# Stick-breaking heads: the suffix products in two one-pass parts

## Chip, cores, metric

The kernel runs on one core of one Trainium2 chip. The metric is the device time of one execution in microseconds (us), the median of several runs. The engines are TensorE (PE: matmuls), VectorE (DVE), ScalarE (ACT), GpSimd (POOL) and SyncE (SP: it issues the loads).

## The reference, cut to what matters

The program is a transformer: a first block, then a second block of two layers, all in float32. The change lies in the first layer of the second block, in the eight heads of the stick-breaking attention:

```python
z = jnp.einsum('bqhd,bshd->bhqs', qb, k, preferred_element_type=F32) * scale
past = key_pos[None, :] < qpos[:, None]
log_keep = jnp.where(past, jax.nn.log_sigmoid(-z), 0.0)
suffix = lax.cumsum(log_keep, axis=3, reverse=True) - log_keep
w = jnp.where(past, jnp.exp(jax.nn.log_sigmoid(z) + suffix), 0.0)
return jnp.einsum('bhqs,bshd->bqhd', w.astype(v.dtype), v)
```

There are 512 positions and 64 channels in a head. The exponent of a weight is z less the sum of softplus(z) over the key itself and all later keys. The same layer also has eight heads of a sparse attention (DSA), which see only the 128 highest-scored keys of each query; choosing them (the top-k) is independent of the stick-breaking heads.

## The kernel before, in words

**Order of work.** Every engine has its own instruction list, written out by hand in one long function, and engines wait for each other on semaphores alone. Nothing is reordered when it runs: an instruction that waits holds up all that stands behind it on its engine.

**The layout of a head.** The scores of a head are held transposed (keys on the 128 partitions, queries along the free axis), in four key tiles. Only queries from the key tile on matter, so they are 512, 384, 256 and 128 columns wide, 1280 in all. They live in PSUM in one of two regions of three banks (`region(h)`, by h % 2). In SBUF, `zw` and `spt` each have two buffers of 128x1280, again by h % 2.

**One head, step by step.**
- `sb_scores(h)` (TensorE, L1106 to L1121): three products of split operands and one mask product for each key tile. It waits until the Exp of head h-2 has read the region, and raises `z_rd`.
- `sb_softplus(h)` (ScalarE, L1757 to L1766): Abs, Exp and Ln, 128x1280 each, into `zw`.
- `sb_max(h)` (VectorE, L2569 to L2573): max(z, 0) + `zw`, which is softplus(z), into `spt`. It waits for the Ln, and for the value products of head h-2 (`sv_rd`), since these read the same buffer of `spt`. It raises `sp_rd`.
- `sb_suffix(h)` (TensorE, L1123 to L1132): ten float32 matmuls with `negtri` (a triangle of -1) or `negone` (all -1) as one operand and `spt` as the other, 2560 columns in all, added onto the scores in PSUM. They wait for `sp_rd` and raise `arg_rd`. The trace shows two matmul records for each.
- The Exp (ScalarE, L1779) reads the region and writes the weights over `spt`; it raises `wgt_rd`.
- `sb_values(h)` (TensorE, L1134 to L1142): twenty products of 64 columns; raises `sv_rd`. `sb_out(h)` (VectorE, L2575 to L2578) copies the result out.

**The lists of the stage.** On TensorE the loop over heads (L1171 to L1187) runs suffix(h), values(h-1), scores(h+2); with h = 1 and 3 transposes of the next pair's queries and keys stand in between (`sb_job`), with h = 5 those of the DSA (`dsa_job`). On ScalarE (L1778 to L1790) it runs Exp(h), then for h = 1, 3, 5 copies that round the transposed queries and keys to the 32-bit matmul format `fp32r` (`sb_high`, `job_high`), then softplus(h+2). On VectorE (L2589 to L2612) it runs max(h+1), the low parts of the queries and keys (`sb_low`), out(h-1), and then up to four rounds of the top-k (`topk`), for h < 4 mixed with `sum_step(13, ...)`, a step of the modulation vectors. The 25 top-k rounds of this loop end in `select`, which writes the last masks `Mk` (L2413) and raises `msk_rd`. Here the loop body of h is called cycle h; on VectorE it begins at max(h+1).

**Ahead of the loop**, ScalarE runs softplus(0), softplus(1), `sb_high(3)` and `split_high(NC1 + 11)` (L1532, the rounded part of a weight chunk that is used after the attention), and VectorE runs max(0), `sb_low(2)`, `sb_low(3)` (L2556, L2557) and `split_low(NC1 + 11)` (L2043).

**Behind the loop** stands the DSA. TensorE runs its first scores, waits for three masks (`msk_rd`, L1227), runs its second scores and then values(7); VectorE follows with the maxima and the copies. The kernel goes on from there with the output projection and the feed-forward layers.

Other products of this kernel already use split operands: ScalarE's Copy into an `fp32r` tile gives the rounded part, and VectorE subtracts that from the full value to give the rest, in `fp32r` too:

```python
A(uH[:, k], X[:, k % 3, :], ACT.Copy)
V.tensor_tensor(uL[:, k], X[:, k % 3, :], uH[:, k].bitcast(F32), ALU.subtract)
```

`overlay` gives out SBUF addresses from the current position and takes none up, so a tile named in it lies on top of what is allocated next.

Of the kernel before, what the change touches and what calls it, by code (L numbers as in the profile page):

```python
# [6 lines left out]
ALU = mybir.AluOpType  # L7
# [141 lines left out]
def program(nc, t, out):  # L149
    ctx = ExitStack()  # L150
    with ctx:
# [8 lines left out]
        with ExitStack() as o:  # L160
# [70 lines left out]
        rp_rd, odd_rp, zero_rd, ixT, ix_hi, ix_lo, ixs_rd, ixr_rd, ix_acc, msk_rd = [sem(n) for n in (  # L231
            "rp_rd", "odd_rp", "zero_rd", "ixT", "ix_hi", "ix_lo", "ixs_rd", "ixr_rd", "ix_acc", "msk_rd")]
        jobT, job_hi, job_lo = sem("jobT"), sem("job_hi"), sem("job_lo")
        z_rd, zmin_rd, zexp_rd, zln_rd, sp_rd, arg_rd, wgt_rd, sv_rd, so_rd = [sem(n) for n in (
            "z_rd", "zmin_rd", "zexp_rd", "zln_rd", "sp_rd", "arg_rd", "wgt_rd", "sv_rd", "so_rd")]
        ds_rd, dmx_rd, dp_rd, dt_rd, dpv_rd, do_rd = [sem(n) for n in ("ds_rd", "dmx_rd", "dp_rd", "dt_rd", "dpv_rd", "do_rd")]
        dpt_rd = [sem("dpt_rd0"), sem("dpt_rd1")]
        aoT, ao_hi, ao_lo = sem("aoT"), sem("ao_hi"), sem("ao_lo")
# [56 lines left out]
        def s2(name, shape, dt=F32):  # L295
# [18 lines left out]
        ixr, = overlay([("ixr", [P, 2, SEQ], F32)])  # L314
        ixH, ixL, izH, izL = overlay([("pad_iz", [P, 1024], F32)] + [(n, [P, 2, SEQ], F32R) for n in
                                                                     ("ixH", "ixL", "izH", "izL")])[1:]
        zw = s2("zw", [P, 2, 1280])
        spt = s2("spt", [P, 2, 1280])
        e2.close()


# [395 lines left out]
        def _(pe):  # L717
# [403 lines left out]
                last.then_inc(z_rd, 1)  # L1121

            def sb_suffix(h):  # L1123
                z, s_ = region(h), spt[:, h % 2]
                pe.wait_ge(sp_rd, h + 1)
                for kt in range(4):
                    for k2 in range(kt, 4):
                        w = SEQ - k2 * P
                        o0 = ZOFF[kt] + (k2 - kt) * P
                        last = mm(z[:, o0:o0 + w], negtri[:] if k2 == kt else negone[:], s_[:, ZOFF[k2]:ZOFF[k2] + w],  # L1130
                                  start=False, stop=True, skip_group_check=True)
                last.then_inc(arg_rd, 1)  # L1132

            def sb_values(h):  # L1134
# [376 lines left out]
        def _(act):  # L1511
# [255 lines left out]

            sb_high(0)
            sb_high(1)
            even_tile_out(4, 0)  # L1770
            sb_softplus(0)
            even_tile_out(4, 2)
# [1 line left out]
            sb_softplus(1)  # L1774
            sb_high(3)
            split_high(NC1 + 11)
            for h in range(NH):
                act.wait_ge(arg_rd, h + 1)  # L1778
                A(spt[:, h % 2], region(h), ACT.Exp).then_inc(wgt_rd, 1)  # L1779
                if h in (1, 3):  # L1780
                    sb_high(h + 3)
                if h == 5:
                    act.wait_ge(z_rd, h + 1)
                    job_high(8, 0, 7, True)
                if h + 2 < NH:
                    sb_softplus(h + 2)
                if h in (1, 3):
                    sb_high(h + 4)
                if h == 5:
                    job_high(9, 0, 7, False)  # L1790
# [241 lines left out]
        def _(dve):  # L2032
# [536 lines left out]
            def sb_max(h):  # L2569
# [2 lines left out]
                    dve.wait_ge(sv_rd, h - 1)  # L2572
                V.scalar_tensor_tensor(spt[:, h % 2], region(h), 0.0, zw[:, h % 2], ALU.max, ALU.add).then_inc(sp_rd, 1)  # L2573

            def sb_out(h):  # L2575
                dve.wait_ge(sv_rd, h + 1)
                V.tensor_copy(T0[:, :, h * HD:h * HD + HD], ps[:, 3, 0:256].rearrange("p (t d) -> p t d", t=4))\
                    .then_inc(so_rd, 1)  # L2578
# [6 lines left out]
            even_tile_out(4, 3)  # L2585
            sb_low(2)
            sb_low(3)
            split_low(NC1 + 11)
            for h in range(NH):  # L2589
                steps = range(TOPK_SB[h], TOPK_SB[h + 1])  # L2590
# [8 lines left out]
                for kt in range(4):  # L2599
                    if h < 4 and kt % 2 == 0:  # L2600
                        sum_step(13, 2 * h + kt // 2)
                    if kt == 1 and h in SB_TURN:
                        group_columns(SB_TURN[h])
                    if kt < len(steps) - 1:
                        topk(steps[kt])
                if h in (1, 3):
                    sb_low(h + 4)
                if h == 5:
# [421 lines left out]
```

## Time and profile before

| | us |
|---|---|
| median of 3 runs | 1778.62 |
| lowest, highest | 1777.19, 1778.79 |
| the profiled execution | 1773.95 |
| its span in the trace | 1772.2 |
| the stage, from the first suffix product to the last mask | 487.7 to 568.0 |

All times below are microseconds from the start of the span of the profiled execution. A view by stretch gives for each engine its busy time and the number of its instructions, then the clock that was granted to TensorE and the DMA load. A timeline row gives start, duration, engine, line, operation, output and inputs with shapes, and in brackets how long the engine had been idle and what released it. The durations of neighbouring VectorE instructions overlap a little, so what an instruction takes from its engine is the distance to the next start where nothing waits.

### The profile page before, as it was taken

Reading aid. Unit: us, or ns where it says so; the run is one execution under the profiler, and the core shown is the slowest. Engines: PE = TensorE matmul, PEld = TensorE weight load, DVE = VectorE, ACT = ScalarE, POOL = GpSimd, SP = SyncE. Lnnn points to the kernel's source line nnn. Section 1 sums busy time; section 2 is a strip of 40 time slices with the busy share of each in tenths; the row PEclk is TensorE's granted clock in tenths of the full one; section 3 lists DMA queues with packets and bytes.
Section 4 is the critical chain, followed back from the end, with each engine's and each line's share of the span. In section 5 each row is a group of like instructions: output and inputs, shape, how many; then the busy total and the mean of one; then the engine's idle time right before and its main releaser. Section 6 shows DMA issues by size and latency. Waiting matters only on the chain.

```text
span 1772.2 us, 22785 instructions
## 1 busy us (share of the span) xinstructions
PE 1666.1 (94%) x8951; PEld 1367.0 (77%) x8957; DVE 1012.6 (57%) x1433; ACT 656.8 (37%) x887; POOL 335.5 (19%) x260
## 2 busy tenths in 40 slices
PE   4999999999988998999999999899879899999999
PEld 3898787888777876888887887677657688888877
DVE  3578798877877758433333447656666733333243
ACT  4422566433363523433332224334453533333121
POOL 0000000000000004788884011224411000000011
PEclk9999999999998998999999999999989999999999
DMA  8645200442210333465554322212002232332321
GB/s 283 202 146 188 95 1 1 135 169 84 83 60 13 96 119 107 147 196 182 185 189 137 118 89 76 96 48 72 24 25 75 64 98 95 97 99 98 118 84 48
DMA packets 145605, 188.00 MB, mean 106 GB/s; under 512 B 6925, under 2 KB 104565, under 8 KB 145524
## 3 DMA queue, kind: packets, MB, share of 16 engines
q1 hardware_dynamic: 145524, 186.88, 32.8%
q8 instruction: 55, 0.90, 0.2%
q14 instruction: 26, 0.21, 0.0%
HBM read 184.77 MB, written 2.10 MB: 105 GB/s over the span
## 4 chain that ended last, share of the span: by engine, by line
PE 59%; DVE 14%; POOL 9%; issue 6%; DMA 5%; ACT 4%; SPq 1%; another core or an unknown queue 0%; POOLq 0%; DVEq 0%; ACTq 0%
PE ps L836 7%; PE ps L837 7%; PE ps L838 7%; POOL mraw L619 4%; POOL msum L626 4%; DMA mraw<-in_w_mod_dram 3%; PE ps L1339 2%; PE ps L1346 2%; PE ps L1340 2%; PE ps L1347 2%; PE ps L1343 2%; PE ps L1348 2%; PE ps L1402 2%; PE ps L1404 2%; PE ps L1403 2%
## 5 line engine op out<-in xcount | busy, mean ns | idle before, releaser
L1532 ACT ACTIVATE whi<-wraw 128x2048 fp32r<-128x2048 f32 x71 | 135.8, 1913 | 312.0 <-PE ps L838 215.4
L2043 DVE TENSOR_TENSOR wlo<-wraw,whi 128x2048 fp32r<-128x2048 f32 x64 | 148.2, 2315 | 154.7 <-ACT whi L1532 154.6
L2794 DVE TENSOR_TENSOR wlo<-wraw,whi 128x2048 fp32r<-128x2048 f32 x22 | 51.7, 2350 | 203.2 <-ACT whi L1892 203.2
L1339 PE MATMUL ps<-uH,whi 128*128 128x512 f32 x352 | 141.4, 402 | 9.8 <-ACT uH L1860 8.3
L836 PE MATMUL ps<-hH,whi 128*128 128x512 f32 x352 | 140.7, 400 | 0.0
L1340 PE MATMUL ps<-uH,wlo 128*128 128x512 f32 x352 | 139.9, 397 | 0.0
L837 PE MATMUL ps<-hL,whi 128*128 128x512 f32 x352 | 139.8, 397 | 0.0
L838 PE MATMUL ps<-hH,wlo 128*128 128x512 f32 x352 | 139.6, 397 | 0.0
L1346 PE MATMUL ps<-uH,whi 128*128 128x512 f32 x352 | 136.9, 389 | 0.0
L1347 PE MATMUL ps<-uL,whi 128*128 128x512 f32 x352 | 136.9, 389 | 0.0
L1348 PE MATMUL ps<-uH,wlo 128*128 128x512 f32 x352 | 136.9, 389 | 0.0
L1343 PE MATMUL ps<-uL,whi 128*128 128x512 f32 x352 | 111.4, 398 | 3.9 <-DVE uL L2733 3.9
L626 POOL TENSOR_TENSOR msum<-msum,mraw 128x512 f32<-128x512 f32 x66 | 107.5, 1628 | 5.2
L836 PE MATMUL ps<-uH,whi 128*128 128x512 f32 x256 | 103.0, 402 | 0.0
L837 PE MATMUL ps<-uL,whi 128*128 128x512 f32 x256 | 100.2, 392 | 0.0
L838 PE MATMUL ps<-uH,wlo 128*128 128x512 f32 x256 | 100.2, 392 | 0.0
L619 POOL TENSOR_TENSOR mraw<-mraw,cpad 128x1024 f32<-128x1024 f32 x44 | 84.9, 1930 | 55.4 <-PE ps L751 42.5
L1896 ACT ACTIVATE whi<-wraw 128x2048 fp32r<-128x2048 f32 x22 | 42.2, 1919 | 138.3 <-PE ps L1348 138.3
L1889 ACT ACT_TABLE_LOAD x22 | 28.2, 1283 | 173.0 <-PE ps L1343 172.9
L2110 DVE SCALAR_TENSOR_TENSOR cy<-utp,cols,cy 128x512 f32<-128x512 f32 x116 | 87.1, 751 | 3.4
L1339 PEld LDWEIGHTS ps<-uH,whi 128*128 128x128 f32 x352 | 67.9, 193 | 26.2 <-issue 12.1
L653 POOL TENSOR_TENSOR sqd<-sqd 128x512 f32<-128x512 f32 x2 | 2.8, 1384 | 434.5 <-ACT sqd L1833 434.5
(500 smaller groups left out, 3910.5 us busy)
## 6 DMA issues: line engine op xcount, KB each, us to landing
mraw<-in_w_mod_dram SPq DMA_DIRECT2D x104, 512.0 KB, 3.8
wraw<-in_w_gate_dram SPq DMA_DIRECT2D x22, 1024.0 KB, 5.3
wraw<-in_w_up_dram SPq DMA_DIRECT2D x22, 1024.0 KB, 5.4
wraw<-in_w_down_dram SPq DMA_DIRECT2D x16, 1024.0 KB, 5.2
wraw<-in_w_in_dram SPq DMA_DIRECT2D x11, 1024.0 KB, 5.4
mfirst<-in_w_mod_dram SPq DMA_DIRECT2D x16, 512.0 KB, 7.5
wraw<-in_w_in_even_dram SPq DMA_DIRECT2D x8, 1024.0 KB, 5.8
wraw<-in_w_in_odd_dram SPq DMA_DIRECT2D x16, 512.0 KB, 4.5
```

The costliest lines, as they stand in the source:

```text
L619: g.tensor_tensor(w, w, cpad[:, 2 * kp:2 * kp + 2, 2:3].to_broadcast([P, 2, GW]), ALU.mult).then_inc(msum_rd, 1)
L626: g.tensor_tensor(msum[:], msum[:], w[:, kk], ALU.add).then_inc(msum_rd, 1)
L836: mm(o, h, xh[:, k0 + k], start=(first and k == 0), stop=False)
L837: mm(o, h, xl[:, k0 + k], start=False, stop=False)
L838: last = mm(o, l, xh[:, k0 + k], start=False, stop=(done and k == nk - 1))
L1339: mm(o[m], w_[0][m][:, k], uH[:, k], start=(k == 0), stop=False)
L1340: mm(o[m], w_[1][m][:, k], uH[:, k], start=False, stop=False)
L1343: last = mm(o[m], w_[0][m][:, k], uL[:, k], start=False, stop=(k == KT - 1))
L1346: mm(o[m], w_[0][m][:, k], uH[:, k], start=(k == 0), stop=False)
L1347: mm(o[m], w_[0][m][:, k], uL[:, k], start=False, stop=False)
L1348: last = mm(o[m], w_[1][m][:, k], uH[:, k], start=False, stop=(k == KT - 1))
L2043: V.tensor_tensor(wlo[:, n % 2, :], wraw[:, n % 2, :], whi[:, n % 2, :].bitcast(F32), ALU.subtract).then_inc(lo_done, 1)
```

## The change

The softplus values `spt` are split before the suffix products. ScalarE copies them to `spH` (type `fp32r`), VectorE subtracts `spH` from `spt` and writes `spL` (also `fp32r`), and TensorE runs the ten suffix matmuls twice, first on `spH`, then on `spL`, with `fp32r` copies of the triangle and of the ones (`rtri`, `rone`). `spH` lies on the addresses of `zw`, `spL` on those of `spt`. The matmuls on `spH` wait for the copy, those on `spL` for the subtraction.

The copy of head h+1 stands on ScalarE behind Exp(h) and the copies that follow it, and ahead of softplus(h+2); that of head 0 stands behind `split_high(NC1 + 11)`. The subtraction of head h+1 stands on VectorE behind the first top-k round of cycle h; that of head 0 stands between `sb_low(3)` and `split_low(NC1 + 11)`. The two small copies `rtri` and `rone` stand on ScalarE behind `sb_high(1)`.

```diff
+        spH, spL = overlay([("spH", [P, 2, 1280], F32R), ("spL", [P, 2, 1280], F32R)])
         zw = s2("zw", [P, 2, 1280])
         spt = s2("spt", [P, 2, 1280])
+        rtri = s2("rtri", [P, P], F32R)
+        rone = s2("rone", [P, P], F32R)
...
             def sb_suffix(h):
-                z, s_ = region(h), spt[:, h % 2]
-                pe.wait_ge(sp_rd, h + 1)
-                for kt in range(4):
-                    for k2 in range(kt, 4):
-                        w = SEQ - k2 * P
-                        o0 = ZOFF[kt] + (k2 - kt) * P
-                        last = mm(z[:, o0:o0 + w], negtri[:] if k2 == kt else negone[:], s_[:, ZOFF[k2]:ZOFF[k2] + w],
-                                  start=False, stop=True, skip_group_check=True)
+                z = region(h)
+                if h == 0:
+                    pe.wait_ge(tri_rd, 1)
+                for part in range(2):
+                    s_ = (spH, spL)[part][:, h % 2]
+                    pe.wait_ge((sph_rd, spl_rd)[part], h + 1)
+                    for kt in range(4):
+                        for k2 in range(kt, 4):
+                            w = SEQ - k2 * P
+                            o0 = ZOFF[kt] + (k2 - kt) * P
+                            last = mm(z[:, o0:o0 + w], rtri[:] if k2 == kt else rone[:], s_[:, ZOFF[k2]:ZOFF[k2] + w],
+                                      start=False, stop=(part == 1), skip_group_check=True)
                 last.then_inc(arg_rd, 1)
...
             sb_high(0)
             sb_high(1)
+            act.wait_ge(rp_rd, 1)
+            A(rtri[:], negtri[:], ACT.Copy)
+            A(rone[:], negone[:], ACT.Copy).then_inc(tri_rd, 1)
             even_tile_out(4, 0)
...
             split_high(NC1 + 11)
+            def sb_part(h):
+                act.wait_ge(sp_rd, h + 1)
+                A(spH[:, h % 2], spt[:, h % 2], ACT.Copy).then_inc(sph_rd, 1)
+
+            sb_part(0)
             for h in range(NH):
                 act.wait_ge(arg_rd, h + 1)
                 A(spt[:, h % 2], region(h), ACT.Exp).then_inc(wgt_rd, 1)
...
+                if h + 1 < NH:
+                    sb_part(h + 1)
                 if h + 2 < NH:
                     sb_softplus(h + 2)
...
+            def sb_rest(h):
+                dve.wait_ge(sph_rd, h + 1)
+                V.tensor_tensor(spL[:, h % 2], spt[:, h % 2], spH[:, h % 2].bitcast(F32), ALU.subtract).then_inc(spl_rd, 1)
...
             sb_low(3)
+            sb_rest(0)
             split_low(NC1 + 11)
             for h in range(NH):
...
                     if kt < len(steps) - 1:
                         topk(steps[kt])
+                    if kt == 0 and h + 1 < NH:
+                        sb_rest(h + 1)
```

## Rows read from the trace of the kernel before

**Rows 1.** Page, section 1: busy time of each engine over the span.

```profile
PE 1666.1 (94%) x8951; PEld 1367.0 (77%) x8957; DVE 1012.6 (57%) x1433; ACT 656.8 (37%) x887; POOL 335.5 (19%) x260
```

**Rows 2.** Busy time by stretch: cycles 1 to 4, cycles 5 and 6.

```profile
505.50:543.30 37.80, 36.23 (x225) 29.10 (x224) 36.56 (x69) 21.46 (x20) 0.00 (x0) 1.00 0.23 70
543.30:568.00 24.70, 21.10 (x129) 17.17 (x127) 20.88 (x39) 9.04 (x9) 0.00 (x0) 0.93 0.00 1
```

**Rows 3.** Waits between 470 and 590 us: who waited for whom; us, times, longest.

```profile
DVE spt L2573 <- PE ps L1141: 5.8, 3, 2.8
...
PE ps L1117 <- DVE uL L2557: 4.6, 2, 4.2
```

**Rows 4.** Timeline of VectorE: start us, duration us, engine, line, operation.

```profile
493.08 0.69 DVE L2557 TENSOR_TENSOR uL<-ps,uH 64x512 fp32r<-64x512 f32 x1
494.32 2.29 DVE L2043 TENSOR_TENSOR wlo<-wraw,whi 128x2048 fp32r<-128x2048 f32 x1 [0.54 <-ACT whi L1532]
496.64 1.49 DVE L2573 SCALAR_TENSOR_TENSOR spt<-ps,zw 128x1280 f32<-128x1280 f32 x1
...
505.54 1.49 DVE L2573 SCALAR_TENSOR_TENSOR spt<-ps,zw 128x1280 f32<-128x1280 f32 x1 [2.73 <-PE ps L1141]
...
525.85 1.49 DVE L2573 SCALAR_TENSOR_TENSOR spt<-ps,zw 128x1280 f32<-128x1280 f32 x1
...
536.99 1.49 DVE L2573 SCALAR_TENSOR_TENSOR spt<-ps,zw 128x1280 f32<-128x1280 f32 x1
...
538.73 0.69 DVE L2398 MAX8 m<-work 128x8 f32<-128x512 f32 x1
...
542.63 0.68 DVE L2400 MATCH_REPLACE8 work<-m,work 128x512 f32<-128x512 f32 x1
546.12 1.49 DVE L2573 SCALAR_TENSOR_TENSOR spt<-ps,zw 128x1280 f32<-128x1280 f32 x1 [2.82 <-PE ps L1141]
...
556.28 1.49 DVE L2573 SCALAR_TENSOR_TENSOR spt<-ps,zw 128x1280 f32<-128x1280 f32 x1 [0.24 <-PE ps L1141]
...
567.56 0.43 DVE L2413 TENSOR_SCALAR Mk<-work 128x512 bf16<-128x512 f32 x1
```

**Rows 5.** Timeline of TensorE, from the score products to the first value products.

```profile
485.16 0.39 PE L1118 MATMUL ps<-uL,uH 128*128 128x512 f32 x1
485.38 0.40 PE L1119 MATMUL ps<-uH,uL 128*128 128x512 f32 x1
...
486.93 0.27 PE L1118 MATMUL ps<-uL,uH 128*128 128x128 f32 x1
487.04 0.28 PE L1119 MATMUL ps<-uH,uL 128*128 128x128 f32 x1
...
487.67 1.02 PE L1130 MATMUL ps<-spt,negtri 128*128 128x512 f32 x2
...
495.69 0.47 PE L1117 MATMUL ps<-uH 128*128 128x512 f32 x1 [3.52 <-ACT spt L1779]
...
498.19 1.12 PE L1130 MATMUL ps<-spt,negtri 128*128 128x512 f32 x2
...
503.06 2.34 PE L1141 MATMUL ps<-T,spt 128*128 128x64 f32 x20
```

**Rows 6.** Timeline of ScalarE around the first head.

```profile
488.70 1.27 ACT L1764 ACTIVATE zw<-zw 128x1280 f32<-128x1280 f32 x1
...
492.38 1.91 ACT L1532 ACTIVATE whi<-wraw 128x2048 fp32r<-128x2048 f32 x1
```

**Rows 7.** TensorE by stretch: length, busy us, granted clock (1.00 is 2.4 GHz, 0.50 is 1.2).

```profile
472.00:476.00 4.00, 1.32 (x3) 0.69 0.00 0
476.00:480.00 4.00, 4.00 (x16) 0.50 0.00 0
492.00:496.00 4.00, 0.48 (x3) 1.00 0.01 2
556.00:560.00 4.00, 2.32 (x6) 0.85 0.01 2
```

More of the change, by code:

```diff
@@ L233, in program @@
         jobT, job_hi, job_lo = sem("jobT"), sem("job_hi"), sem("job_lo")
-        z_rd, zmin_rd, zexp_rd, zln_rd, sp_rd, arg_rd, wgt_rd, sv_rd, so_rd = [sem(n) for n in (
-            "z_rd", "zmin_rd", "zexp_rd", "zln_rd", "sp_rd", "arg_rd", "wgt_rd", "sv_rd", "so_rd")]
+        z_rd, zmin_rd, zexp_rd, zln_rd, sp_rd, arg_rd, wgt_rd, sv_rd, so_rd, sph_rd, spl_rd, tri_rd = [sem(n) for n in (
+            "z_rd", "zmin_rd", "zexp_rd", "zln_rd", "sp_rd", "arg_rd", "wgt_rd", "sv_rd", "so_rd", "sph_rd", "spl_rd", "tri_rd")]
         ds_rd, dmx_rd, dp_rd, dt_rd, dpv_rd, do_rd = [sem(n) for n in ("ds_rd", "dmx_rd", "dp_rd", "dt_rd", "dpv_rd", "do_rd")]
```

## Prediction

> **What bounds the kernel now.** I read four views in this order. The page says that TensorE is busy for 94% of the span [rows 1], which invites the thought that any TensorE time saved is time saved. So the busy time by stretch comes next. The stage with the suffix products runs from 487.67 [rows 5] to the last mask, which ends at 567.99 (567.56 + 0.43) [rows 4]. In its middle, 505.5 to 543.3, VectorE is busy 36.56 us of 37.8 and TensorE 36.23: two engines are full at once. Behind it, to 568.0, VectorE has 20.88 of 24.7 [rows 2]. The waits tell which is the limit where. VectorE waited for value products three times in the stage, 5.8 us together [rows 3], and the timeline puts these waits at the starts of cycles 1, 5 and 6 (2.73, 2.82 and 0.24 us ahead of max). Between 505.54 and 543.31 (542.63 + 0.68) it had none [rows 4]. So cycles 1 to 4 are VectorE's. The stage itself ends when VectorE has finished its top-k: the DSA's second scores wait for the last mask, and values(7), and all later work, stand behind them on TensorE. Whatever VectorE does more in a full cycle shifts that mask.
>
> TensorE spends on one suffix stream, with four transposes behind it, 4.87 us (498.19 to 503.06) [rows 5], about 4.4 without them. That is what the change shortens.
>
> **The change part by part.**
>
> *The suffix streams.* With `fp32r` operands, score matmuls start 0.22 us apart at 512 columns and 0.11 apart at 128 [rows 5]. For 384 and 256 I take 0.17 and 0.14, a little under and about on the straight line. One stream has 1, 2, 3 and 4 matmuls of 512, 384, 256 and 128 columns: 0.22 + 0.34 + 0.42 + 0.44 = 1.4 us. Two streams take 2.8 in place of 4.4, so TensorE saves 1.6 us a head, 13 in all. In the cycles that VectorE fills this is worth nothing.
>
> *The copy on ScalarE.* SBUF to SBUF, 1280 columns, costs 1.27 us as Exp [rows 6]. The PSUM variants are no dearer, so both ends lie at about 1.25 and I take 1.27. In a cycle it lies beside TensorE's score products. These take 2.5 us (495.69 to 498.19) [rows 5] and begin no later than max does, so the high stream starts some 3.0 us after max starts (1.49 + 0.1 + 1.27 + 0.1; 0.1 is my estimate of a hand-over, of which the trace shows 0.03 from 494.29 on ScalarE [rows 6] to 494.32 on VectorE [rows 4]). Behind the copy only softplus(h+2) is queued. It ends at about 6.8, which is long ahead of the next max. The two small copies ahead of the loop fall where ScalarE has time, and I cost them at nothing. Without that cover they would cost two instructions well under 1.27.
>
> *The subtraction on VectorE.* It has not run at this size. The nearest row above is max itself: two inputs, 1280 columns, 1.49 us. The subtraction of 2048 columns takes 2.29 and one of 512 takes 0.69 [rows 4], and the line between these gives 1.49 again. Starts follow some 0.07 sooner than ends, so I take 1.42 a piece. As a lower bound I use 0.8, should 1280 columns run at about half that price. The upper bound is 1.5.
>
> *The head of the stage.* Before, suffix(0) could start at 487.67, as soon as softplus was there. Now the copy of head 0 stands on ScalarE behind `split_high`, which ends at 494.29 [rows 6]. The copy ends at 495.6. TensorE has nothing to do for 8 us, from about 487.6 to 495.7. The longest wait for L2557, 4.2 us [rows 3], ends in the stretch from 472 to 476, where the granted clock was 0.69; over the next 4 us it was 0.50, the 1.2 GHz level. The wait of 3.52 us ahead of 495.69 [rows 5] left it at 1.00 [rows 7]. An idle time of 8 is beyond both, so I take suffix(0) at the low clock: 2 x 2.8, end at 501.3. Then Exp(0) to 502.65 and score products to 505.25. Suffix(1) takes 2.8 to 508.05, the transposes 0.45, the value products 2.34 [rows 5], and max(2) starts at 510.95 where it started at 505.54 [rows 4]: **+5.4**. At full clock suffix(0) ends at 498.5 and all this comes 2.7 sooner. VectorE doesn't set it: the subtraction of head 0 ends at 497.1, `split_low` 2.3 later, max(1) at 500.85, and what is left of cycle 0 is done by 508.5.
>
> *Cycles 1 to 3* took 31.45 us (505.54 to 536.99) [rows 4] without idle time and get one subtraction each: **+4.3**.
>
> *Cycle 4.* VectorE reached 543.31 and waited until 546.12. Now the chain runs: max and the copy out 1.74, one top-k round 1.52 (a third of the 4.58 from 538.73 to 543.31) [rows 4], subtraction 1.49, hand-over 0.1, low stream 1.4, transposes 0.45, value products 2.34. The sum is 9.05, against 9.13 before: **-0.1**. Here the shorter streams pay for the subtraction and the wait for it.
>
> *Cycles 5 and 6* are full once the 0.24 us wait is gone: 2 x 1.42 - 0.24 = **+2.6**. In each full cycle the low stream waits for the subtraction, about 5 us after max starts, but TensorE then has 2 to 3 us in hand before the next max needs its buffer.
>
> *Behind the stage* nothing changes, and nothing there has the time to absorb a late mask, so the shift stays. No transfer is added or moved, and SP's and POOL's lists are unchanged.
>
> **The sum:** 5.4 + 4.3 - 0.1 + 2.6 = +12.2 us. The profiled execution took 1773.95, so its like would take 1786.1. That execution lies 4.7 under the median of 1778.62. Against the median the sum gives 1790.8, and that is my number.
>
> **A rule on the clock.** The Trainium skill, page "TensorE: Matmul & The Clock Gate", section "HAM oscillation — how this bites in real kernels", says that a loop with an idle wait in each round can find its matmuls slowed in each round. By it the sum would be that of the second rival below. The trace agrees in part: the idle time of 3.52 us left the clock alone, the 4.2 did not.
>
> **The rivals.**
>
> *No fall at the head.* Suffix(0) runs at full clock. For it speaks the wait of 3.52 us that left 1.00 [rows 7]; against it, that the new one is over twice as long. 12.2 - 2.7 = +9.5: 1788.1.
>
> *A fall in every cycle.* In each cycle TensorE would be idle for 2 to 4 us in several pieces. Over 556 to 560, with 2.32 us busy of 4, the clock went down to 0.85 [rows 7], so short pieces can do it. A fall as at 472 to 480 lasts (0.31 + 0.50) x 4 / 0.5 = 6.5 us and costs TensorE half of that, 3.2. In cycles 1 to 3 and 5 some 2.5 of it are covered, which leaves 0.6 each. In cycle 4 nothing is covered. That adds 4 x 0.6 + 3.2 = 5.6, for +17.8: 1796.4. Against it speaks that over all of cycles 1 to 4 the clock stood at 1.00 [rows 2], though with fuller work.
>
> *TensorE is the limit, and the kernel gets faster.* The place is the start of a cycle, max(h+1) behind the value products. If the shorter streams took away the three waits of 5.8 us [rows 3], and the subtractions and the head fell into time that VectorE has over, the mask would come 5.8 us sooner: 1772.8. It decides where VectorE is idle for more than 1.42 us in a cycle. It was so in cycles 0 and 4 alone, and the head delay takes the first.
>
> *The shift is taken up later.* Some wait behind the mask, on a transfer or on ScalarE, would have to be as long as 12 us. It would give 1778 to 1781. None of the views read shows one.
>
> *The streams are not one-pass.* If a matmul with `fp32r` copies took as long as one with float32, both streams would cost 4.4. The chain of a cycle would then be 12 us or more, the head over 6 more, about +23 in all: 1802. The score matmuls' 0.22 us speaks against it.
>
> **How the numbers follow.** Forecast 0.43, no fall 0.22, a fall in every cycle 0.19, faster 0.05, taken up later 0.07, not one-pass 0.04. The range begins at the case without a fall with cheaper subtractions (9.5 less 5 x 0.6 = 6.5, so 1785) less 1 for the scatter of the runs (1777.19 to 1778.79): 1784. It ends at the fall in every cycle with the same scatter: 1798. A measurement can tell about 0.2%, 3.6 us, from no change. With 0.01 moved to each of the first two from the slower cases, which hold 0.88, faster by more has 0.06, within has 0.08, slower has 0.86.
>
> **What would show it.** Right: the two suffix streams of a head at 1.4 us each at full clock. Subtractions of 1.49 us, eight of them. The first suffix matmul at 495.7 with a granted clock near 0.5. Cycle 1 beginning at about 511, cycles 1 to 3 of 11.5 to 12.6 us with no idle time on VectorE, and the last mask at about 580. The head step is wrong if the clock over 496 to 501 is 1.00 (mask at about 577.5). The step on the full cycles is wrong if max waits for value products again in cycles 2, 3 or 4: then the chain over ScalarE and TensorE is longer than I have it. The whole is wrong if the mask is late and the end is not.

## Result and profile after

The changed kernel takes 1791.23 us in the median of 4 runs (1788.30 to 1792.39); the kernel before, timed beside it, 1777.90 (1775.05 to 1778.79). The ratio is 1.0076, with a 95% interval from 1.0059 to 1.0092: 13 us slower. The profiled execution took 1792.3 us, its span 1790.5.

The page of the changed kernel, section 1, answers to [rows 1]:

```profile
PE 1670.1 (93%) x8957; PEld 1374.6 (77%) x8957; DVE 1023.9 (57%) x1441; ACT 667.1 (37%) x897; POOL 333.1 (19%) x260
```

TensorE is busy for 4 us more (1666.1 before), though its streams are cheaper; a busy time counts matmuls at the low clock at their full length. VectorE has 11.3 us more (1012.6 before) and ScalarE 10.3 (656.8). These are the eight subtractions, which take 1.41 us each from VectorE's time (8 x 1.41 = 11.3), and the ten copies, whose durations add up to 10.8 us and overlap their neighbours a little.

VectorE's timeline of the changed kernel answers to [rows 4]; L2591 is max, L2595 the subtraction, L2431 the mask:

```profile
487.82 1.49 DVE L2591 SCALAR_TENSOR_TENSOR spt<-ps,zw 128x1280 f32<-128x1280 f32 x1 [5.53 <-ACT zw L1773]
...
500.22 1.49 DVE L2595 TENSOR_TENSOR spL<-spt,spH 128x1280 fp32r<-128x1280 f32 x1 [1.70 <-ACT spH L1790]
...
503.95 1.49 DVE L2591 SCALAR_TENSOR_TENSOR spt<-ps,zw 128x1280 f32<-128x1280 f32 x1
...
508.22 1.49 DVE L2595 TENSOR_TENSOR spL<-spt,spH 128x1280 fp32r<-128x1280 f32 x1 [1.26 <-ACT spH L1790]
...
515.19 1.49 DVE L2591 SCALAR_TENSOR_TENSOR spt<-ps,zw 128x1280 f32<-128x1280 f32 x1 [2.44 <-PE ps L1148]
```

```profile
550.84 1.49 DVE L2591 SCALAR_TENSOR_TENSOR spt<-ps,zw 128x1280 f32<-128x1280 f32 x1
...
554.09 1.49 DVE L2595 TENSOR_TENSOR spL<-spt,spH 128x1280 fp32r<-128x1280 f32 x1
...
560.01 1.49 DVE L2591 SCALAR_TENSOR_TENSOR spt<-ps,zw 128x1280 f32<-128x1280 f32 x1 [1.46 <-PE ps L1148]
...
571.36 1.49 DVE L2591 SCALAR_TENSOR_TENSOR spt<-ps,zw 128x1280 f32<-128x1280 f32 x1
...
584.05 0.43 DVE L2431 TENSOR_SCALAR Mk<-work 128x512 bf16<-128x512 f32 x1
```

The subtraction takes 1.49 us, and the next instruction starts 1.41 later (501.63, 509.63 in the same view). The subtractions of heads 0 and 1 wait for their copies (1.70 and 1.26 us); no later one does. Read the starts of max as the beats of the stage. The third of them is the start of cycle 1, the sixth (550.84) that of cycle 4. Max never waits between 515.19 and 550.84; it waits for value products (L1148) at cycles 1 and 5, and no longer at cycle 6. The parts of the stage, from the start of max(0) to the end of the last mask:

| part of the stage (us) | before | predicted change | changed | measured change | second trace of the changed kernel |
|---|---|---|---|---|---|
| head, max(0) to max(2) | 22.25 | +5.4 | 27.37 | +5.12 | 27.02 |
| cycles 1 to 3 | 31.45 | +4.3 | 35.65 | +4.20 | 35.64 |
| cycle 4 | 9.13 | -0.1 | 9.17 | +0.04 | 9.19 |
| cycles 5 and 6, to the mask | 21.87 | +2.6 | 24.47 | +2.60 | 24.46 |
| stage | 84.70 | +12.2 | 96.66 | +11.96 | 96.31 |

TensorE's timeline shows the two streams, first of head 0, then of head 1, then of head 2; it answers to [rows 5]:

```profile
500.34 0.76 PE L1137 MATMUL ps<-spH,rtri 128*128 128x512 f32 x1 [7.76 <-ACT spH L1790]
...
502.92 0.73 PE L1137 MATMUL ps<-spL,rtri 128*128 128x512 f32 x1
...
509.47 0.47 PE L1137 MATMUL ps<-spH,rtri 128*128 128x512 f32 x1
...
510.88 0.44 PE L1137 MATMUL ps<-spL,rtri 128*128 128x512 f32 x1
...
518.04 0.50 PE L1137 MATMUL ps<-spH,rtri 128*128 128x512 f32 x1
...
520.98 0.50 PE L1137 MATMUL ps<-spL,rtri 128*128 128x512 f32 x1 [1.34 <-DVE spL L2595]
```

In head 1 the streams start 1.41 us apart, the predicted 1.4. In head 0 they start 2.58 apart, after 7.76 us of idle time. In head 2 the second one waits 1.34 us for VectorE, as predicted for the full cycles. The clock over the head, in pieces of 4 us (length, busy, granted clock), answers to [rows 7]:

```profile
492.00:496.00 4.00, 0.58 (x6) 0.93 0.00 0
496.00:500.00 4.00, 0.00 (x0) 0.50 0.00 0
500.00:504.00 4.00, 3.66 (x14) 0.50 0.02 4
504.00:508.00 4.00, 2.58 (x13) 0.79 0.00 0
```

It is at 0.50, the level of 1.2 GHz, from before 496 until after 504, where the kernel before had 1.00.

**Where the rest of the 18 us between the two profiled executions is.** The difference of their spans is 18.3 us. max(0) starts at 487.82 and not at 483.29: 4.5 us, all of it ahead of the stage, where only the two small copies (0.6 us) are new. In the second trace of the changed kernel it starts at 483.12, so this is scatter between executions. The stage gives 11.96. From the mask to the last output copy of the DSA it is 61.27 against 60.03: 1.2, which goes with the clock, as the traces below show. The rest, 0.6, lies behind. The medians, 13.3 apart, agree with stage and tail together.

### The profile page after: what moved, and what is told of

It is laid out like the page before. It is cut to its first block, busy times and chain, and to the rows that moved or that the text cites. A ratio compares the mean times of both kernels' runs of the same rounds, so it can differ in the third digit from the quotient of the medians.

```text
span 1790.5 us, 22816 instructions
## 1 busy us (share of the span) xinstructions
PE 1670.1 (93%) x8957; PEld 1374.6 (77%) x8957; DVE 1023.9 (57%) x1441; ACT 667.1 (37%) x897; POOL 333.1 (19%) x260
## 4 chain that ended last, share of the span: by engine, by line
PE 60%; DVE 14%; POOL 9%; issue 7%; DMA 4%; ACT 4%; SPq 1%; POOLq 0%; DVEq 0%; ACTq 0%
PE ps L839 7%; PE ps L841 7%; PE ps L840 7%; POOL mraw L622 4%; POOL msum L629 4%; DMA mraw<-in_w_mod_dram 3%; PE ps L1346 2%; PE ps L1353 2%; PE ps L1355 2%; PE ps L1347 2%; PE ps L1350 2%; PE ps L1354 2%; PE ps L1409 2%; PE ps L1411 2%; PE ps L1410 2%
## 5 line engine op out<-in xcount | busy, mean ns | idle before, releaser
L1346 PE MATMUL ps<-uH,whi 128*128 128x512 f32 x352 | 140.9, 400 | 10.6 <-ACT uH L1878 8.3
```

The costliest lines, as they stand in the source:

```text
L1346: mm(o[m], w_[0][m][:, k], uH[:, k], start=(k == 0), stop=False)
```

## Experiments

All times of parts are read from VectorE's timeline as in the table above. "Stage" is from the start of max(0) to the end of the last mask, "tail" from there to the last output copy of the DSA.

| kernel | head | cycles 1-3 | cycle 4 | cycles 5, 6 | stage | tail | median of runs |
|---|---|---|---|---|---|---|---|
| before | 22.25 | 31.45 | 9.13 | 21.87 | 84.70 | 60.03 | 1777.9 to 1779.5 |
| changed | 27.37 | 35.65 | 9.17 | 24.47 | 96.66 | 61.27 | 1791.2 |
| changed, second trace | 27.02 | 35.64 | 9.19 | 24.46 | 96.31 | 61.17 | 1790.1 (one run) |
| split of head 0 forward | 22.26 | 35.66 | 10.17 | 24.46 | 92.55 | 61.07 | 1787.5 |
| no subtractions | 26.41 | 31.76 | 9.09 | 21.65 | 88.91 | 57.06 | 1781.3 |
| second stream unread | 27.44 | 35.64 | 12.26 | 24.46 | 99.80 | 62.16 | 1794.7 |
| second stream cut | 25.72 | 35.64 | 12.80 | 24.45 | 98.61 | 61.32 | 1792.1 |
| second stream cut, again | 25.98 | 35.65 | 7.91 | 24.45 | 93.99 | 60.94 | 1786.1 (one run) |
| TensorE kept busy in the head | 26.00 | 35.66 | 12.25 | 24.46 | 98.37 | 62.06 | 1789.1 |
| subtractions on GpSimd | 23.28 | 34.17 | 10.37 | 21.65 | 89.47 | 62.69 | 1786.2 |
| float32, rounds moved | 23.47 | 29.26 | 9.78 | 18.83 | 81.34 | 58.64 | 1771.0 |
| float32, rounds moved, Exp first | 20.55 | 29.27 | 9.78 | 18.83 | 78.43 | 56.86 | 1768.0 |
| split, rounds moved | 23.52 | 32.97 | 10.02 | 20.38 | 86.89 | 56.90 | 1779.4 |
| split, rounds moved, Exp first | 21.53 | 36.22 | 10.18 | 20.40 | 88.33 | 57.50 | 1775.6 |

**The head: the place of the first copy.**

```diff
             sb_high(2)
+            sb_part(0)
             sb_softplus(1)
             sb_high(3)
             split_high(NC1 + 11)
-            sb_part(0)
...
             sb_low(2)
+            sb_rest(0)
             sb_low(3)
-            sb_rest(0)
             split_low(NC1 + 11)
```

> The changed kernel with the split of head 0 moved forward: its copy stands on ScalarE ahead of softplus(1), its subtraction on VectorE ahead of the low parts of the keys. I measure the stage from the start of max(0) to the end of the last mask: 84.70 us in the kernel before, 96.66 in the changed one. My theory (VectorE's list is the limit in the full cycles, and the head is late because the copy stands behind the weight split): suffix(0) ends before Exp(0) can run anyway, so the head costs nothing, max(2) comes 22.3 us after max(0) (27.4 in the changed kernel, 22.3 before), the clock stays at full speed over the head, and the stage takes 91.6. Whole time some 5 us under the changed kernel, 8 over the one before. Rival (the place of the copy does not matter, TensorE and ScalarE wait for each other in every cycle alike): stage within 1 us of 96.7.

The head fell to 22.26 us, that of the kernel before to 0.01. The ratio to the kernel before is 1.0036 (1.0025 to 1.0048), against 1.0076. So the +5.1 goes away with the place of the first split (its copy and its subtraction). The stage came out at 92.55 and not 91.6, since cycle 4 took 1.0 us more; in this trace TensorE's clock was 0.50 from 545 to 548, in the midst of it. The clock over the head stayed at full speed only until 492, and that part of the expectation was wrong:

```profile
487.00:492.00 5.00, 3.57 (x29) 1.00 0.02 3
492.00:497.00 5.00, 1.27 (x3) 0.65 0.00 0
...
545.00:548.00 3.00, 3.00 (x14) 0.50 0.00 0
```

The agreement to 0.01 us is a balance of two differences, and luck. After a wait of 5.16 us for Exp(0) the score products ran at the low clock: 4.37 us (495.73 to 500.10), against 2.50 in [rows 5].

```profile
495.70:500.30 4.60, 4.57 (x17) 0.50 0.00 0
```

```profile
495.73 0.77 PE L1120 MATMUL ps<-uH 128*128 128x512 f32 x1 [5.16 <-ACT spt L1795]
...
500.10 0.60 PE L1137 MATMUL ps<-spH,rtri 128*128 128x512 f32 x1
```

```profile
498.21 1.27 ACT L1787 ACTIVATE spH<-spt 128x1280 fp32r<-128x1280 f32 x1 [2.62 <-DVE spt L2591]
```

So suffix(1) started 16.39 us after max(0), and 14.90 after it in the kernel before: 1.49 later. Its two streams took 2.93 us (to 503.03) where the float32 stream took 4.44 (498.19 to 502.63): 1.51 shorter. Up to 0.6 of the 1.49 is the clock. The other 0.9 is the copy of head 1, which ended at 499.48 (498.21 + 1.27), so no score product could have brought suffix(1) ahead of that. Here the shorter streams pay for the new copy on the path, and for the low clock.

**VectorE's time: with and without subtractions.**

```diff
-                    s_ = (spH, spL)[part][:, h % 2]
-                    pe.wait_ge((sph_rd, spl_rd)[part], h + 1)
+                    s_ = spH[:, h % 2]
+                    pe.wait_ge(sph_rd, h + 1)
...
-            sb_rest(0)
...
-                    if kt == 0 and h + 1 < NH:
-                        sb_rest(h + 1)
```

> The changed kernel without the eight subtractions: the second stream reads the rounded part again, so the remainder is left out and the rounded part counts twice. All copies and all matmuls stay. My theory: cycles 1 to 3 go back to 31.5 us together (35.65 in the changed kernel), cycle 4 takes 8.7 (9.17), cycles 5 and 6 take 21.6 (24.47), the head stays late, so the stage takes 89.1, 7.5 less than the changed kernel. Rival (the loss is in TensorE's idle waits for the copies and in its clock, not in VectorE's time): the cycles stay at over 11 us each and the stage at 94 or more.

Stage 88.91 against 89.1 expected; the parts missed by more than the sum, the head by -0.9 us, cycles 1 to 3 by +0.3 and cycle 4 by +0.4. TensorE and ScalarE had the work of the changed kernel, copies and both streams, and still cycles 1 to 3 went back to 31.8 us. The ratio to the kernel before is 1.0011 (0.9994 to 1.0028). Its counterpart keeps the subtractions too, and only lets the second stream read the rounded part:

```diff
-                    s_ = (spH, spL)[part][:, h % 2]
-                    pe.wait_ge((sph_rd, spl_rd)[part], h + 1)
+                    s_ = spH[:, h % 2]
+                    if part == 0:
+                        pe.wait_ge(sph_rd, h + 1)
                     for kt in range(4):
+                        if part and kt == 3:
+                            pe.wait_ge(spl_rd, h + 1)
```

> The changed kernel with all copies, subtractions and both full streams, but the second stream reads the rounded part again, and only its last matmul waits for the subtraction; the remainder is left out and the rounded part counts twice. Against the run without subtractions it differs by VectorE's work alone. My theory: cycles 1 to 3 take 35.65 us and cycles 5 and 6 take 24.46, as in the changed kernel (31.76 and 21.65 without subtractions). Cycle 4 tells about the miss with the cut second stream (12.80 us where 7.9 was expected): there the clock stood at 0.50, and here TensorE has 1.3 us more work in each head with the same waits. If the clock was the cause, cycle 4 takes 7.9 to 9.2. Rival (a wait that I don't see): 12.8 again.

Cycles 1 to 3 took 35.64 us and cycles 5 and 6 took 24.46, the changed kernel's numbers. Between these two runs lie 3.9 us over three cycles and 2.8 over two, that is 1.3 to 1.4 for each subtraction, and 1.41 is what one takes from VectorE's time. This is the clearest pair of the study: same matmuls, same copies, and the subtractions on VectorE make the difference. (The last matmul of a head waits for its subtraction here, but max never waited for value products in cycles 1 to 3, so that wait was not on the path.) Cycle 4, however, took 12.26 us and not 7.9 to 9.2, with TensorE busy throughout at a clock of 0.61.

**TensorE's time: a shorter second stream.**

```diff
                         for k2 in range(kt, 4):
+                            if part and kt < 3:
+                                continue
```

> The changed kernel with the second stream cut to its last matmul, of 128 columns: the remainder of three key tiles of four is left out. Copies and subtractions stay. This takes about 1.3 us of TensorE from each head (2.4 from head 0, at the low clock). My theory: nothing changes in cycles 1, 2, 3, 5 and 6; the head gets 3.7 to 3.9 shorter and cycle 4 gets 1.3 shorter, so the stage takes 91.5. Rival (TensorE's streams are on the path in every cycle): each head gives 1.3 and more, 10 to 11 in all, and the stage takes 86.

Cycles 1, 2, 3, 5 and 6 didn't move by more than 0.02 us, though TensorE had 1.3 us less work in each. Its time didn't fall with the work: over cycles 1 to 3 it was busy for 28.31 us at a clock of 0.77, against 26.61 at 0.99 in the changed kernel. That the beat held even so shows that TensorE's time doesn't set it, and the rival of a gain in every head falls. But two parts missed. The head gave 1.65 us, not 3.7: the score products started 2.4 us sooner and suffix(1) took 1.3 less, but the score products ran at the low clock and took 4.34 us (502.45 to 506.79) instead of 2.36 (507.11 to 509.47 in the changed kernel). Cycle 4 got 3.6 us longer where it should have got 1.3 shorter. VectorE's row says for whom it waited, and the windows say why that was late:

```profile
559.70 1.49 DVE L2593 SCALAR_TENSOR_TENSOR spt<-ps,zw 128x1280 f32<-128x1280 f32 x1 [4.95 <-PE ps L1150]
```

```profile
546.90:550.00 3.10, 3.10 (x15) 0.50 0.00 0
550.00:553.00 3.00, 3.00 (x14) 0.50 0.00 0
553.00:556.00 3.00, 3.00 (x16) 0.50 0.03 5
556.00:559.70 3.70, 3.70 (x18) 0.50 0.00 0
```

TensorE was busy all the time in cycle 4, at half clock from end to end. The same kernel once more, to see whether that belongs to it:

> The kernel with the cut second stream once more, unchanged: does the long cycle 4 come again? The remainder of three key tiles of four is left out. If the clock falls wherever TensorE has too little to do in the full cycles: cycle 4 above 11 us again and the granted clock near 0.5 in it. If it was chance in one execution: 7.9 to 9.2.

```profile
544.75:552.66 7.91, 7.88 (x58) 0.88 0.00 0
```

```profile
544.75 1.49 DVE L2593 SCALAR_TENSOR_TENSOR spt<-ps,zw 128x1280 f32<-128x1280 f32 x1
...
552.66 1.49 DVE L2593 SCALAR_TENSOR_TENSOR spt<-ps,zw 128x1280 f32<-128x1280 f32 x1 [0.20 <-PE ps L1150]
```

Cycle 4 took 7.91 us, the 7.9 worked out from rows, at a mean clock of 0.88. The very same instructions had taken 12.80 at 0.50, with TensorE busy in both all the time. So the clock is worth 4.9 us in this cycle, and its price is shown by one program with itself. What decides between the two is not settled: nothing in the program differs. One thing did repeat: over cycles 1 to 3 the clock was 0.77 and 0.74 in the two traces of the cut stream, 0.99 in both of the changed kernel, and 0.89 to 0.95 in the three others with two full streams and the same rounds. Over whole executions it was 0.953 to 0.961 in the six runs of the one and 0.963 to 0.968 in the five of the other. So with less work on TensorE the clock was lower each time; it costs time only where TensorE sets the beat.

**Keeping TensorE busy in the head.**

```diff
             sb_job(3)
+            pe.wait_ge(job_lo, 3)
+            for _ in range(32):
+                mm(ps[:, 7, :], uH[:, 1, 0:P], uH[:, 0, :], start=True, stop=True)
             for h in range(NH):
                 sb_suffix(h)
```

> The changed kernel with 32 matmuls of 512 columns into a bank that nobody reads, on TensorE ahead of suffix(0), where it waits for the copy: some 7 us of work that fills the idle time. My theory: the clock stays at full speed, suffix(0) takes 2.8 us and not 5.3, max(2) comes 2.4 to 2.7 us sooner, and the stage takes 94.1. Rival (the late head is a matter of order alone, the clock costs nothing): stage 96.7. If the filling runs longer than the wait, suffix(0) starts later than 12.5 us after max(0), and I count that off.

```profile
487.65 7.54 PE L1180 MATMUL ps<-uH 128*128 128x512 f32 x32
495.66 0.47 PE L1137 MATMUL ps<-spH,rtri 128*128 128x512 f32 x1 [0.47 <-ACT spH L1793]
...
497.10 0.51 PE L1137 MATMUL ps<-spL,rtri 128*128 128x512 f32 x1
...
500.12 0.58 PE L1120 MATMUL ps<-uH 128*128 128x512 f32 x1 [1.42 <-ACT spt L1798]
...
504.04 0.47 PE L1137 MATMUL ps<-spH,rtri 128*128 128x512 f32 x1
```

It did what it was to do and gained little. The filling ran from 487.65 to 495.2, the two streams of suffix(0) start 1.44 us apart instead of 2.58, and over 496 to 500 the clock is 1.00. But then TensorE waits for Exp(0) for 1.42 us, and now the clock falls there, to 0.56: the score products take 3.92 us (500.12 to 504.04), against 2.50 in [rows 5]. In the changed kernel the same wait of 1.42 us stands ahead of score products that ran at 1.00, so its length alone doesn't decide. The head got 1.4 us shorter, not 2.4 to 2.7: 2.3 from the streams and 0.6 from an earlier start of suffix(0) after max(0) (11.90 us against 12.52), less the 1.4 of the slow score products and 0.1 that I can't place. Against the second trace of the changed kernel (27.02) it is 1.0. Cycle 4 took 12.25 at a clock of 0.61, and the stage got longer. In this one trace, filling one idle time moved the fall and didn't avoid it.

**A second trace of the changed kernel.**

> The changed kernel once more, for a second trace of it: what the order of work sets should repeat to 0.1 us (cycles 1 to 3 35.65, cycles 5 and 6 24.47), and what the clock sets may not (the head of 27.4, cycle 4 of 9.2, the time behind the mask). My theory: head 26 to 27.5, cycle 4 between 9.2 and 12.8. Rival (the clock has no part): all four repeat to 0.1 us.

All parts of the stage repeated, to 0.35 us in the head and to 0.02 in the rest; I had expected more scatter in head and cycle 4. The fall in the head is thus part of this program's behaviour, and cycle 4 of the changed kernel came out at 9.2 twice. Whether it ever takes 12 there, as in one trace each of three relatives, stays open with two traces.

**GpSimd in VectorE's place.** With the split of head 0 forward:

```diff
+            pool.wait_ge(zero_rd, 8)
+            for h in range(1, NH):
+                pool.wait_ge(spl_rd, h)
+                pool.wait_ge(sph_rd, h + 1)
+                g.tensor_tensor(spL[:, h % 2], spt[:, h % 2], spH[:, h % 2].bitcast(F32), ALU.subtract).then_inc(spl_rd, 1)
...
-                    if kt == 0 and h + 1 < NH:
-                        sb_rest(h + 1)
```

> The changed kernel with the split of head 0 moved forward and the subtractions of heads 1 to 7 on GpSimd, which has nothing to do in this stage. Nothing is left out. A GpSimd operation of 512 columns takes 1.3 us and one of 1024 takes 1.9 to 2.8 in the kernel before, so I take 3.0 for 1280. My theory: VectorE's cycles fall back to those of before, and the chain over ScalarE and GpSimd takes 10 to 10.6 us a cycle, with cycle 4 at about 10.6 to 11: stage 87 us, 9 to 10 under the changed kernel and 2 over the one before. Rival (the two engines get in each other's way, or GpSimd takes much longer than 3 us): operations of VectorE longer than before and a stage over 92.

```profile
499.42 2.93 POOL L657 TENSOR_TENSOR spL<-spt,spH 128x1280 fp32r<-128x1280 f32 x1 [12.67 <-ACT spH L1793]
509.73 2.94 POOL L657 TENSOR_TENSOR spL<-spt,spH 128x1280 fp32r<-128x1280 f32 x1 [7.38 <-ACT spH L1793]
520.12 2.93 POOL L657 TENSOR_TENSOR spL<-spt,spH 128x1280 fp32r<-128x1280 f32 x1 [7.45 <-ACT spH L1793]
```

```profile
500.75 2.15 DVE L2338 SCALAR_TENSOR_TENSOR msum<-mraw,cpad,msum 128x512 f32<-128x512 f32 x1
...
509.13 0.74 DVE L2338 SCALAR_TENSOR_TENSOR msum<-mraw,cpad,msum 128x512 f32<-128x512 f32 x1
...
512.28 0.93 DVE L2338 SCALAR_TENSOR_TENSOR msum<-mraw,cpad,msum 128x512 f32<-128x512 f32 x1
...
522.26 1.00 DVE L2433 TENSOR_SCALAR ptd<-score,m 128x384 f32<-128x384 f32 x1
```

GpSimd took 2.93 us, as estimated, and cycles 5 and 6 fell to 21.65. Cycles 1 and 2 took 10.39 and 10.80, near the chain of 10 to 10.6. The third took 12.98, with TensorE's clock at 0.74 over it and at 1.00 over the two before. The stage was 89.47, between theory (87) and rival, 7.2 us under the changed kernel and 4.8 over the one before. The fair counterpart is the kernel with the split of head 0 forward alone (stage 92.55): against that the stage gave 3.1 us and the whole nothing. It stood at 1.0040 (1.0026 to 1.0054) times the kernel before, the other at 1.0036. There is some contention, too: a scalar-tensor-tensor operation of VectorE that takes 0.74 us otherwise took 2.15 and 0.93 when it met a subtraction on GpSimd, and a tensor-scalar of 384 columns took 1.00, where the kernel before has 0.42. All three ended soon after GpSimd did. The first two ended 0.55 and 0.54 us after it (502.90 against 502.35, 513.21 against 512.67), the last 0.21 (523.26 against 523.05). The Trainium skill, page "SBUF — State Buffer", section "SBUF: two separate sides", says that the two engines share a pair of ports that one instruction holds to its end. The three rows agree with it, if only the part of an instruction that grows with its columns has to wait. That part can be estimated from this case's rows: VectorE's subtraction takes 0.69 us for 512 columns and 1.49 for 1280, so 512 columns alone take 0.53; a tensor-scalar of the kernel before takes 0.42 for 384 columns and 0.49 for 512, so 384 columns alone take 0.21. By these estimates the instructions outlasted GpSimd by just that part.

**VectorE relieved: eight top-k rounds ahead of the loop.** The predicted limit gives a forecast for the old kernel as well: it should get faster if VectorE's rounds move to where it waits.

```diff
-            (4, 0): range(20, 21), (4, 1): range(21, 23)}
-TOPK_SB = (23, 26, 30, 33, 37, 40, 44, 48, 48)
+            (4, 0): range(20, 21), (4, 1): range(21, 27), (4, 2): range(27, 31)}
+TOPK_SB = (31, 32, 34, 38, 40, 44, 46, 48, 48)
...
             sb_low(2)
+            topks(4, 2)
             sb_low(3)
```

> The kernel before (float32 suffix products) with eight of the 25 top-k rounds moved ahead of the loop, four ahead of max(0) and four ahead of the low parts of the keys, where VectorE waited 5.5 and 5.9 us; the 17 others are spread anew. Nothing is left out. My theory (VectorE was the limit in cycles 1 to 3 and at the end): TensorE's chain of score products, suffix and value products sets the cycles now, 9.3 to 10.3 us each, the last cycle takes 8.7, max(2) stays 22.3 us after max(0), and the stage takes 78.9 us where it took 84.7: the whole 5 to 6 us faster. Rival (TensorE was the limit all along): stage 84 to 85, no gain.

The median was 1770.98 us, ratio 0.9955 (0.9942 to 0.9969). The stage took 81.34, not 78.9: 1.2 of the miss are in the head (clock 0.93 over it), and 1.3 in cycles 1 to 5, which the expectation doesn't divide further. In cycles 1 to 3 TensorE was busy for 29.08 us of 29.26 at a clock of 1.00, and VectorE now had idle time: it waited twice, 3.7 us together, for the rounded halves of queries and keys. So there the limit had passed to TensorE, as the theory said:

```profile
513.37 0.68 DVE L2556 TENSOR_TENSOR uL<-ps,uH 64x512 fp32r<-64x512 f32 x1 [1.99 <-ACT uH L1742]
...
532.45 0.68 DVE L2556 TENSOR_TENSOR uL<-ps,uH 64x512 fp32r<-64x512 f32 x1 [1.75 <-ACT uH L1742]
```

The whole gained 7 us where the stage gave 3.4; 1.4 more came in the tail, and I can't place the other 2.2. The same move with the split:

> The changed kernel with the split of head 0 moved forward, as in the first experiment, and with the same eight top-k rounds ahead of the loop and the same new spread. Nothing is left out. If relieving VectorE let the shorter streams pay, this would beat the kernel with float32 products and the same spread. My theory: it doesn't. The chain of a cycle over max, a top-k round, the subtraction, the low stream and the value products is 9.3 to 9.9 us, no shorter than TensorE's chain with float32 products, and VectorE has 9.9 us more to do: stage 82.6 us, some 3.7 longer than with float32 products. Rival (the streams pay once VectorE has room): stage under 78.

1779.43 us, ratio 1.0011 (0.9992 to 1.0031). The stage took 86.89 us, not 82.6, and is 5.55 longer than with float32 products (I had 3.7): 3.71 in cycles 1 to 3, 0.24 in cycle 4, 1.55 in cycles 5 and 6, and nothing in the head. Max waited for value products again at cycles 4, 5 and 6 (1.31, 0.79 and 1.03 us). So in these cycles it is the chain over VectorE, ScalarE and TensorE that takes the time, no longer VectorE's full list alone. Giving VectorE room didn't turn the shorter streams into time. Then the other thing that the kernel before shows in [rows 5], the wait of 3.52 us for Exp(0):

```diff
             sb_high(3)
-            split_high(NC1 + 11)
             for h in range(NH):
                 act.wait_ge(arg_rd, h + 1)
                 A(spt[:, h % 2], region(h), ACT.Exp).then_inc(wgt_rd, 1)
+                if h == 0:
+                    split_high(NC1 + 11)
...
-            split_low(NC1 + 11)
             for h in range(NH):
                 steps = range(TOPK_SB[h], TOPK_SB[h + 1])
                 if h + 1 < NH:
                     sb_max(h + 1)
+                if h == 0:
+                    split_low(NC1 + 11)
```

> As the kernel with float32 products and eight rounds ahead, and with Exp(0) on ScalarE ahead of the weight split (on VectorE its second half behind max(1)). In the kernel before, TensorE waited 3.5 us for this Exp. My theory: the head gets 1.9 us shorter (max(2) 20.4 us after max(0)), the stage takes 77.0. Rival (something else holds the second score products, such as the low parts of the keys): no change against the kernel with the rounds alone.

```profile
504.56 1.49 DVE L2574 SCALAR_TENSOR_TENSOR spt<-ps,zw 128x1280 f32<-128x1280 f32 x1 [0.18 <-PE ps L1141]
```

```profile
562.01 0.43 DVE L2414 TENSOR_SCALAR Mk<-work 128x512 bf16<-128x512 f32 x1
```

The head took 20.55 us against 20.4 expected, the stage 78.43 against 77.0; the miss is that of the run before with float32 products, in cycles 1 to 6. The whole took 1768.03 us in the median, ratio 0.9935 (0.9916 to 0.9954): 10 us faster than the kernel before, 23 faster than the changed one, with the float32 products kept and nothing left out. And the split with all three moves:

> The split with all that I found to help: split of head 0 moved forward, eight top-k rounds ahead of the loop, Exp(0) ahead of the weight split on ScalarE. Nothing is left out. Its counterpart with float32 products took 78.4 us for the stage and 1768.0 in all. My theory: the split has no place in which it pays: max(2) comes 22.5 us after max(0) (20.6 with float32 products), the stage takes 85.9, and the whole some 8 us more than the counterpart, 1776. Rival (its loss was only the bad places of copy and rounds): within 2 us of the counterpart.

1775.62 us, ratio 0.9990 (0.9980 to 1.0000). That is 7.6 us more than its counterpart, as forecast (8). The stage, however, took 88.33 and not 85.9, so the fit of the whole is partly luck. The head took 21.5 and cycles 1 to 3 took 36.2, with one of them at 13.45, at a clock of 0.67, and 0.81 over the three, against 1.00 with float32 products. The same cycles took 32.97 without the move of Exp(0), at 0.94. Of the 6.95 us more than with float32 products, then, 3.7 came also in the run before, and 3.25 go with the clock.

## Why the prediction was right

**The limit.** "Cycles 1 to 4 are VectorE's" was read from 36.56 us busy of 37.8 [rows 2] and from the rows of max without a bracket [rows 4]. The pair with and without the subtractions shows it: same TensorE and ScalarE work, 35.64 against 31.76. The run with rounds moved shows it from the other side: with fewer rounds in the loop cycles 1 to 3 took 29.26 and not 31.45. One word is too much in it: the idle time ends at 543.31, so cycle 4 was full only to there, as the sum had it.

**The streams.** 1.4 us predicted, 1.41 measured at full clock. At the low clock 2.58 and not 2.8, since I doubled the whole 1.4 and not the columns' share alone. TensorE's saving of 1.6 us a head was counted as nothing in the full cycles, and cutting the second stream moved them by no more than 0.02.

**The subtraction.** 1.42 taken, 1.41 measured. Cycles 1 to 3: +4.20 for +4.3. Cycles 5 and 6: +2.60 for +2.6.

**The head.** +5.12 for +5.4. Both halves are shown: the order (moving the first split gives 5.1 back), and the clock (0.50 from 496 to 504). What the prediction didn't ask is what the head costs with a better order. There the shorter streams gave 1.5 us, and the copy of head 1 and the low clock took them away again. The share that I gave to the clock, 2.7, is confirmed only in part. The two slow streams cost 2 x (2.58 - 1.41) = 2.3 us; but when I kept the clock up by filling, the next idle time took 1.4 of it, and the net gain was 1.4.

**Cycle 4.** +0.04 for -0.1: max to max over copy, first round, subtraction, second stream and value products. The clock was 0.86 over the cycle, at 0.50 only until about 553. That it held in two traces of two owes something to luck, since four traces of its relatives show 10.2 to 12.8 us for the same chain or a shorter one.

**Behind the stage.** "The shift stays" held. What I had not seen is that the tail has a clock term of its own: 57 to 59 us in the five traces in which the clock stood at 1.00 for 12 us behind the mask, 60 to 62.7 where it was 0.50 to 0.72. The kernel before was among the latter. So 1.2 us of the difference between the two profiled executions lies there. The link to the clock is a correlation over fourteen traces; no run changed the tail alone. And the number, 1790.8 for 1791.23, is nearer than its parts: the difference was 13.3 us and not 12.2, and the kernel before ran 0.7 us faster beside it than the 1778.62 that I started from.

**The rivals.** "No fall at the head" is out: the fall is in both traces. "A fall in every cycle" did not come in the changed kernel, but its price in cycle 4 was near, and was paid by its relatives: I gave a fall in the uncovered cycle 4 a cost of 3.2, and the two with full streams and the fall took 3.1 more than 9.17, the cut stream 3.6 more (4.9 more than its own second trace), while their cycles 1 to 3 stayed at 35.65. In cycles 1 to 3 I had counted 0.6 each for falls, and down to a clock of 0.74 they cost nothing: the cover was larger than I made it. "TensorE is the limit" is out by the run with the cut stream. "Not one-pass" is out by the 1.41 us of a stream. "The shift is taken up later" is out: the whole is 13.3 us longer, stage and tail 13.2.

**The rule on the clock.** The Trainium skill's page "TensorE: Matmul & The Clock Gate", section "HAM oscillation — how this bites in real kernels", which ties slowed matmuls to idle waits that recur, did no harm to the sum: over cycles 1 to 3 of the changed kernel TensorE was busy for 26.61 us of 35.65, and the clock was 0.99. In other kernels with the split it was 0.74 to 0.95 over these cycles. The traces here neither confirm it as a rule nor rule it out.

## What to carry to other kernels

Before you make one engine's work cheaper, look for the engine whose instructions follow each other without a gap, and count what the cheaper form hands to it: here two streams saved TensorE 1.6 us a head and put 1.41 on VectorE, which had none to give. A new step on an in-order queue costs what stands ahead of it, and some 5 of the 12 us lost in the stage came from one split that stood behind a weight split. The same reading says where the real gain lies: work of the full engine that can move into its own idle times, ahead of the loop, which gave 7 us and then 10.

## What the runs showed of the hardware

- The same program took 12.80 and 7.91 us for one cycle, at granted clocks of 0.50 and 0.88. A stretch in which TensorE's chain sets the time differed by up to 4.9 us between two executions, and one in which another engine sets it did not (35.64 to 35.66 us in seven traces, at clocks from 0.74 to 0.99). Parts of a stage, cut at the full engine's instructions, compare to 0.02 us where whole times scatter by 4.
- Less work on TensorE went with a lower clock: 0.77 and 0.74 over cycles 1 to 3 with the second stream cut, 0.89 to 0.99 in five traces with both full streams. Behind a filled wait the score products took 3.92 us instead of 2.50. The length of the wait ahead doesn't tell: after 3.52 us the clock was 1.00, after 5.16 it was 0.50, and after 1.42 it was 1.00 in one kernel and 0.56 in another. What sets the moment of a fall stays open.
- GpSimd needs 2.93 us for a float32 subtraction of 128x1280, VectorE 1.49. Three VectorE operations that met it took 2.15 and 0.93 us instead of 0.74, and 1.00 instead of 0.42, and ended 0.55, 0.54 and 0.21 us after GpSimd; others, such as MAX8, kept their 0.55.
